# Expert stage of a streaming encoder step: the order of gathers and scatters on POOL, and of copies and casts on ACT

## The reference, cut to what matters

```python
act = silu(einsum('bnd,edf->bnef', h, w_g)) * einsum('bnd,edf->bnef', h, w_u)
out = einsum('bnef,efd->bnd', act * comb[..., None], w_d)     # comb: 2 experts of 32 per token
```

## Time and profile before

| What | Value |
|---|---|
| Median of 3 runs | 1278.8 us (1276.46 to 1279.06) |
| The profiled execution's own time | 1278.63 us |
| Its span in the trace | 1276.8 us |
| Busy: PE, DVE, ACT, POOL | 96%, 72%, 40%, 35% of the span |
| Granted TensorE clock, mean | 0.988 of full speed |
| DMA traffic | 163.84 MB, mean 128 GB/s |
| Expert stage in the trace | about 1043 to 1236 us |

### The profile page before, as it was taken

The page is one execution under the profiler, slowest core; times in us unless marked ns, Lnnn a source line. Parts: engine busy times, 40 slices in busy tenths (PEclk is TensorE's granted clock), DMA queues, the critical chain, the costliest instruction groups (busy, mean ns, idle before and its releaser), DMA issues.

```text
span 1276.8 us, 21392 instructions
## 1 busy us (share of the span) xinstructions
PE 1223.0 (96%) x7563; PEld 1066.7 (84%) x7563; DVE 918.7 (72%) x2179; ACT 512.2 (40%) x1117; POOL 440.9 (35%) x740
## 2 busy tenths in 40 slices
PE   6999999999999999998999999999999979998995
PEld 6999999999999999998777667999788858887752
DVE  5657888888999998884667776332666668886747
ACT  6655223232322112324656564100432247765634
POOL 5803575666774115654000000210011233432320
PEclk9999999999999999999999999999999989999998
DMA  7201332222213221102000131944221469999749
GB/s 270 75 30 53 92 72 80 43 79 42 71 43 124 86 84 53 35 1 94 11 1 17 44 98 55 344 133 164 116 83 49 151 228 340 359 341 338 294 165 374
DMA packets 79456, 163.84 MB, mean 128 GB/s; under 512 B 12417, under 2 KB 48081, under 8 KB 78209
## 3 DMA queue, kind: packets, MB, share of 16 engines
q1 hardware_dynamic: 64977, 128.84, 29.8%
q0 software_dynamic: 12656, 27.62, 6.5%
q10 hardware_dynamic: 1728, 6.10, 1.2%
HBM read 137.86 MB, written 39.21 MB: 139 GB/s over the span
## 4 chain that ended last, share of the span: by engine, by line
PE 82%; DMA 7%; DVE 3%; POOL 2%; ACT 2%; SPq 2%; issue 1%; POOLq 0%; ACTq 0%; DVEq 0%
PE bank L921 12%; PE bank L922 12%; PE bank L923 12%; PE bank L1134 5%; DMA region_h<-in_wd 4%; PE bank L1116 3%; PE bank L1218 3%; PE bank L1212 3%; PE bank L1350 3%; PE bank L1052 2%; PE bank L1229 2%; PE bank L1230 2%; PE bank L1231 2%; DMA region_q<-expert_rows_scratch 2%; PE bank L1214 2%; PE bank L1365 1%
## 5 line engine op out<-in xcount | busy, mean ns | idle before, releaser
L1968 DVE MAX8 small<-region_kv 128x8 f32<-128x272 f32 (+4 forms) x241 | 190.2, 828 | 47.6 <-DVE region_kv L1973 47.5
L921 PE MATMUL bank<-h_hi,w_hi 128*128 128x384 f32 (+1 forms) x576 | 196.1, 340 | 0.0
L922 PE MATMUL bank<-h_lo,w_hi 128*128 128x384 f32 (+1 forms) x576 | 196.0, 340 | 0.0
L1973 DVE MATCH_REPLACE8 region_kv<-small,region_kv 128x272 f32<-128x272 f32 (+4 forms) x241 | 195.5, 819 | 0.0
L923 PE MATMUL bank<-h_hi,w_lo 128*128 128x384 f32 (+1 forms) x576 | 194.4, 338 | 0.0
L921 PE MATMUL bank<-w_hi,h_hi 128*128 128x256 f32 x448 | 128.8, 288 | 1.0 <-ACT region_q L1518 1.0
L2331 POOL TENSOR_TENSOR w_lo<-w_stage,w_hi 128x512 fp32r<-128x512 f32 x64 | 80.8, 1293 | 140.6 <-ACT w_hi L1457 140.5
L923 PE MATMUL bank<-w_hi,h_lo 128*128 128x256 f32 x448 | 125.9, 281 | 0.0
L922 PE MATMUL bank<-w_lo,h_hi 128*128 128x256 f32 x448 | 125.9, 281 | 0.0
L923 PEld LDWEIGHTS bank<-h_hi,w_lo 128*128 128x128 f32 x576 | 108.7, 189 | 0.0
L922 PEld LDWEIGHTS bank<-h_lo,w_hi 128*128 128x128 f32 x576 | 108.2, 188 | 0.6
(11 more groups left out here) (350 smaller groups left out, 3061.2 us busy)
## 6 DMA issues: line engine op xcount, KB each, us to landing
w_stage<-in_w_in SPq DMA_DIRECT2D x72, 256.0 KB, 3.2
region_kv<-in_xa SPq DMA_DIRECT2D x16, 512.0 KB, 6.1
region_h<-in_wg SPq DMA_DIRECT2D x15, 512.0 KB
region_h<-in_wu SPq DMA_DIRECT2D x15, 512.0 KB
region_h<-in_wd SPq DMA_DIRECT2D x15, 512.0 KB
region_q<-in_wd SPq DMA_DIRECT2D x12, 512.0 KB
region_q<-in_wg SPq DMA_DIRECT2D x12, 512.0 KB
region_q<-in_wu SPq DMA_DIRECT2D x12, 512.0 KB
```

The lines of the kernel that those rows point to most:

```text
L921: mm(out, st_hi(k), mv_hi(k), start=(k == 0), stop=False)
L922: mm(out, st_hi(k), mv_lo(k), start=False, stop=False)
L1968: nc.vector.max(m8[:, q, :], x).then_inc(dve_c, 1)
L1973: nc.vector.match_replace(x, m8[:, q, :], x, TAKEN).then_inc(dve_c, 1)
```

## The change

Two orders are changed, and nothing else: no instruction is added, removed or resized, and no wait is added or removed.

```diff
@@ ACT, expert loop
                 silu_e(e % 2)
                 if e + 1 < NE:
                     rows_upper(e + 1)
-                if e + 2 < NE:
-                    expert_upper(e + 2)
                 act.wait_ge(act_turned, e + 1)
                 if e >= 2:
                     act.wait_ge(dn_done, e - 1)
                 cp(actT[:, e % 2, :], bank[6 + e % 2][:, 2 * P:3 * P]).then_inc(actT_ready, 1)
+                if e + 2 < NE:
+                    expert_upper(e + 2)
                 if e >= 1:
                     second_half(e - 1)
             second_half(NE - 1)
@@ POOL, expert loop
             list_out(NT - 1)
-            for e in range(NE + 1):
+            for e in range(NE + 2):
                 if e + 3 < NE:
                     pool.wait_ge(te_done, 2 * (e + 1))
                     gather(hg[:, e % 3, :], gidx[:, e + 3:e + 4], hg_in[e % 3])
-                if e >= 1:
-                    y = e - 1
+                if e >= 2:
+                    y = e - 2
                     pool.wait_ge(y_ready, y + 1)
                     pool.wait_ge(y_act, y + 1)
                     scatter(ysb[:, y % 3, :], heads[:, y, 0:1], y_out[y % 3])
```

## The result

| | before | after |
|---|---|---|
| median, 17 runs each on one chip | 1277.95 us | 1279.85 us |
| ratio, 95% interval | | 1.0014 [1.0007, 1.002] |
| profiled execution: time, span | 1278.63, 1276.8 | 1279.85, 1278.0 |
| first gather to SiLU of expert 31 | 190.4 | 192.2 |

The kernel became 0.14% slower, 1.8 us by the ratio. That is less than the 0.2% set as what a measurement can tell, yet 17 runs a side put its interval on the slower side of 1.

The account below looks back on a forecast made before the run. PE was taken to bound the first stretch, weight loads through SP's full queue the second. -0.36 (copy) + 1.48 (gather) - 1.1 (hole) = 0.0 us, with 0.17 us for the median gives 1278.7; range 1275.3 to 1281.0.

Parts of the forecast that it names:

- The gather ahead of the weights of 30: Late in the expert stage, the last gather goes out 8.7 us earlier, ahead of those weights: +1.48 us.
- lists on half of the engines: Late loads: lists of 72 rows of 128 fit only about half the DMA engines being busy, supporting 1.48 us.
- the order in the queues: DMA queues: round-robin keeps the 1.48 us price, sum 0.0; strict arrival order puts the last gather behind every load, sum -1.46.
- The credit of 1.1 us: Stage start, 1057 to 1060 us, DMA share 0.63: an earlier gather pushes weights into this hole, -1.1 us.
- ACT's order in the first stretch: While PE sets the pace, casts start 1.46 us later but PE's beat stays 5.58 us: cost 0, gain 0.
- The copy at the end: Expert 28's copy no longer waits for the casts of 30, so the turn of 29 starts earlier: -0.36 us.
- The rows that PE waited for: Second stretch: PE's 5.4 us of waits for gathered rows; taking them away gives nothing by itself.
- (a): Rival, faster: loads speed up in the second stretch, 3.0 us plus the copy's 0.36, so 1275.3; chance 0.16.
- (b): Rival, slower: the hole gives nothing, two gathers' traffic precedes the weights of 30, +2.6, so 1281.3; chance 0.12.
- (c): Rival: the gather goes out earlier but lands when it did, only the copy's 0.36 comes, 1278.4; chance 0.10.
- my marks: Signs in POOL, ACT, DMA share and late casts, such as gather +0.3 us after the turn, casts within 1 us of 1215.04.
- the 0.62: Chance of no change in the sum's own form, 1277.3 to 1280.3 us.

Follow-up runs that it names:

- its late half alone: POOL's new order from the 17th expert on only, ACT as before, against the kernel before: 1278.88 us, ratio 1.0013.
- the dealt rows: Each expert's list places dealt over all partitions: on the kernel before 1277.68 us, ratio 1.0001; on the changed kernel 1280.64 us, ratio 1.0024.
- late loads: The kernel before with three extra unused 512 KB loads in SP's queue, behind gate/up loads of experts 15, 20 and 25: 1281.36 us, ratio 1.0034.
- second half first: ACT does copy, second half, then casts: with POOL's old order 1277.38 us, ratio 0.9997; with POOL's new order 1279.02 us, ratio 1.0009.
- its copy: The changed kernel measured once more on another chip, against the kernel before: 1280.23 us, ratio 1.002.
- four buffers: Four gather buffers, POOL's new order, ACT with copy, second half, casts: 1277.75 us, ratio 1.0005; with the last two gathers at old places 1275.78 us, 0.9987.
- ten in the middle: POOL's new order for gathers 20 to 29 only, ACT as before, against the kernel before: 1278.59 us, ratio 1.0004.
- a fourth buffer: POOL's new order with a fourth gather buffer, each gather a beat earlier still, ACT as before, against the kernel before: 1276.82 us, ratio 0.9994.

## Why the prediction was wrong

It said "no change", 1278.7 us, with 0.12 on slower. The time of 1279.85 lies in the range; against the 1277.95 of its own comparison it is +1.8, where the sum was 0.0. The measured move is inside the 0.2% that I had called no change, but its sign is not zero, and these terms carry it.

**The gather ahead of the weights of 30: right in size, not shown in kind.** Bounds of 0.83 and 1.48 us, 1.48 taken. POOL's order alone gave +1.2, its late half alone +1.7, and late bytes cost what their size says; these numbers don't choose between the two ends. That it is the last gather that costs isn't shown: moved back in the changed kernel, the last two saved 0.3. The lead was less than I said: by the stage's own clock the last gather went out 4.1 us earlier (1208.61, before 1213.68), not 8.7, as a scatter that itself waits for ACT stands ahead of it. The reason that I gave for it, lists on half of the engines, has the dealt rows against it. As for the order in the queues: coming behind every load, the moved gather would have made POOL's order a gain; it cost 1.2 to 1.7. This is what the Trainium skill ("DMA: Bandwidth & Descriptors", Queues, rings and completion order) would have: each engine goes round-robin between the queues it has work for, so a gather takes its turns at once. How far this holds for each engine no run here shows.

**The credit of 1.1 us: a step that failed.** "I take 1.1, since the DMA share reads near 1 on both sides of the hole." The window did fill, 0.99 for 0.63, but three microseconds of one execution are a poor gauge, as the stage's start differs by up to 2.5 us from run to run: with late loads the same window reads 0.85, with POOL's old order. Taken 19 to 22 us after the first gather it reads 0.66 before, 0.67, 0.76, 0.78 and 0.83 in four more kernels whose early gathers have the old order (late loads, rows dealt out, second half first, POOL's order late), 0.87 with POOL's order alone and 0.87 and 0.91 in the change and its copy. So the hole was filled by a half or so, and it did not last: 1.1 us at 355 GB/s would be 0.39 MB, and by 60 us from the first gather the change had moved 21.60 MB against 21.54, by 120 us 42.03 against 42.68. POOL's order alone had 21.66 and 42.48. What else was put in early came back in part at most: 1.8 of 4.4 us for three loads, 0 of 1.5 for a down weight. Without the credit the forecast's own terms make +1.1.

**ACT's order in the first stretch, costed at nothing: the other step that failed, by about 1 us.** All that I worked out for ACT came true to a tenth: it idles 1.19 us, casts start 1.46 later, SiLUs stay 5.58 apart. I then wrote "The scatter moves by 1.3 us with the second half; its buffer is taken again three beats (16.7 us) after." and "POOL itself: cost 0." That priced the scatter as work for POOL and not as traffic. Its new place is right behind the loads of gate and up. There the loads' packets take longer from 45 to 60 us (184 ns against 173 with POOL's order alone), and SP's long issues follow each other 21 us sooner than before, while POOL's order alone has them from 1124.4 on; in the four other kernels with this place of the scatter and POOL's new order they do so 5 to 19 us sooner. The price of ACT's order beside POOL's new one can be read five times: 0.6 and 1.4 us (the change and its copy against POOL's new order with the second half first) and 1.9 (rows dealt out against POOL's order alone, one chip) on three buffers, 0.9 (one chip) and 2.3 on four. All five have one sign, and none is clear of both intervals by itself. That the scatter's place behind the loads is what costs, by way of slower packets, fits all of the runs but was argued: it never moved alone, as the gather moves with it, to 2.06 us after the SiLU in place of 1.6, right behind the scatter.

**The copy at the end: right in kind, half the size.** The down product of 28 was not over before the weights landed, as I had it: PE was still at the products of 29 and started it 2.0 us after. The turn of 29 did wait for DVE's product, as I had said, and starts 3.71 us after the cast of 30, where I had 3.67 and the kernel before 4.03. But the products of 30 follow the turn later than they did before, which the forecast left out; after and before:

```profile
1219.79 0.32 PE L1375 MATMUL bank<-consts,region_t 128*128 128x128 f32 x1
1220.05 0.35 PE L1365 MATMUL bank<-expert_high,rowsT_hi 128*128 128x256 f32 x1
```

```profile
1219.16 0.36 PE L1365 MATMUL bank<-expert_high,rowsT_hi 128*128 128x256 f32 x1
```

That is 0.26 us behind the turn in place of 0.09, and from the cast of 30 to the SiLU of 31 the gain was 0.18 us, not 0.36.

**The rows that PE waited for: right.** They were worth nothing, in the change and in POOL's order alone.

**The rivals.** (a), faster loads: the share from 1160 to 1180 us did rise from 0.92 to 0.95, but it fell from 0.97 to 0.95 in the stretch before; by the packets' records 20.43 MB moved from 60 to 120 us after the first gather (before 21.14), and 13.68 from 120 to 160 (before 13.24): the later stretch gained less than the earlier one had lost. (b), slower: the side was right and its "if the hole gives nothing" too; its mechanism, two gathers ahead of the last weights, is not what happened, as moving the last two back in the changed kernel saved 0.3 us. One of its numbers is off: 2.96 us are 2.0 gathers of 1.48, not 1.9. (c) has the rows against it: the gathers' lead filled the window. Of my marks, the gather was to stand 0.3 us behind the turn of the rows; it stands 1.2 behind, as the scatter at 1085.11 is ahead of it. The casts of 30 started 1.04 us after 1215.04 (2.0 by the stage's own clock), where 1 was the bound, and the share did leave 0.92, upwards. The lower end of the 0.62 should have been 1277.6: 1278.7 less 0.6 and 0.5.

So 1.1 (the forecast's sum without the credit, the copy in it at 0.36) + about 1 (ACT's order) makes +2.1, beside 1.8 and 2.6 measured. The second term is a mean of readings from 0.6 to 2.3, so this sum is no proof.

**What stays open.** Which gathers carry POOL's 1.2 us. The last two matter on four buffers (+0.6 against -1.7 us, intervals touching at the edge) and hardly in the changed kernel (2.3 against 2.6), and ten in the middle gave +0.5 with an interval that holds both. Why a fourth buffer is worth about 2 us on POOL's new order. Why early bytes don't count in full. And whether the scatter's new place, the gather's or their standing back to back is what slows the loads.

## What to carry to other kernels

When a transfer's issue moves, look up which other transfers go out within a microsecond of its new place, even on an engine that has slack: here the order on ACT that moved a scatter by 1.3 us cost 0.6 to 2.3 us by its readings, about as much as the order of the gathers. A hole in a DMA share is no credit until the bytes moved over the whole stretch have been counted; the price of bytes in the bound stretch may be worked out, a credit far ahead of it may not. And the halves of a change don't add: ACT's order alone cost 2.6 us and POOL's 1.2, the whole 1.8 to 2.6, since POOL's half takes away the waits that ACT's half alone runs into.

## What the runs showed of the hardware that was not expected

- Loads late in a stage with a full queue cost their size, 4.3 us [2.7, 6.0] for 1.57 MB; the same loads at its start still cost 2.6 [1.5, 3.7].
- The mean duration of a 4 KB packet of SP's queue, 45 to 60 us after the first gather, was 179 to 190 ns with a scatter issued 0.4 us behind two loads, and 167 to 174 ns with it elsewhere in the beat.
- After SP's last issue the loads run at about half of the DMA share (0.49 to 0.57 between 1205 and 1215 us in 17 of the 20 traces, 0.40 to 0.45 in three), wherever the rows lie. Why is open.
- In the first stretch POOL's scatter took 1.48 us to issue in its old place and 1.01 in its new one, with the gathers at 1.00 in both. With the second half first and POOL's old order it was 1.01 for the scatter and 2.02 for the gather. POOL had idle time for all of it.
